# Expert items of 32 slots in four column tiles instead of 64 slots in two, rows gathered for four items at a time as before

## The reference, cut to what matters

```
def hierarchical_moe(xn, rg_w, rg_b, re_w, re_b, w1, w3, w2):
    ...
    g_top, g_idx = lax.top_k(g_prob, 1)                      # one of 4 groups
    ...
    e_top, e_idx = lax.top_k(jax.nn.softmax(e_logits), 2)    # two of its 8 experts
    e_w = e_top / jnp.sum(e_top, axis=-1, keepdims=True) * g_top
    ...
    h = jax.nn.silu(jnp.einsum('td,edf->tef', t, w1)) * jnp.einsum('td,edf->tef', t, w3)
    h = h * gate[:, :, None].astype(h.dtype)
    y = jnp.einsum('tef,efd->td', h, w2)
```

```
11  6  4  1 13  3 13  3 |  8  5  5  6 10 11  3 12
65 10 25 40 44 57 43 62 |  4  3  3 15  3  8  2 14
```

## Time and profile before

| | us |
|---|---|
| median of 3 runs | 1420.75 (1420.71 to 1421.07) |
| span of the profiled execution | 1421.0 |
| TensorE busy / DVE / ACT / GpSimd | 1355.8 / 537.2 / 347.3 / 228.6 |
| moved from HBM | 468.95 MB |

### The profile page before, as it was taken

One profiled execution on the slowest core, in us unless ns is written; L12 is line 12 of the kernel. 1 busy time (PEld: TensorE's weight loads), 2 busy tenths in 40 slices (PEclk: granted clock), 3 DMA queues, 4 the chain that ended last, 5 costly groups with the idle time before them and its releaser, 6 DMA issues.

```text
span 1421.0 us, 19044 instructions
## 1 busy us (share of the span) xinstructions
PE 1355.8 (95%) x7236; PEld 766.4 (54%) x7236; DVE 537.2 (38%) x1017; ACT 347.3 (24%) x623; POOL 228.6 (16%) x205
## 2 busy tenths in 40 slices
PE   7999999999999999998998999999999999898987
PEld 7884898987786345444433533544544543443533
DVE  6999420544425233233313323223323331331315
ACT  1121378566571111110210110111111121111003
POOL 2002756687881000000000000000000000000000
PEclk9999999999999999999999999999999999999999
DMA  8433543434475999999999999959999999999993
GB/s 214 178 119 119 208 178 119 155 142 161 140 292 235 384 428 428 427 428 427 428 429 428 429 428 428 428 224 429 428 428 428 428 428 428 429 428 428 428 425 138
DMA packets 71540, 471.76 MB, mean 332 GB/s; under 512 B 17329, under 2 KB 17410, under 8 KB 46274
## 3 DMA queue, kind: packets, MB, share of 16 engines
q1 hardware_dynamic: 70834, 469.75, 80.5%
q10 hardware_dynamic: 528, 1.05, 0.2%
q0 software_dynamic: 128, 0.26, 0.1%
HBM read 468.95 MB, written 2.10 MB: 331 GB/s over the span
## 4 chain that ended last, share of the span: by engine, by line
PE 62%; DMA 19%; DVE 2%; ACT 1%; issue 1%; POOL 1%; DVEq 0%; POOLq 0%; SPq 0%; ACTq 0%
PE ps L1932 24%; DMA ring<-in_expert_w_dram 18%; PE ps L1950 12%; PE ps L1590 11%; PE ps L1910 5%; PE ps L1940 3%; PE ps L1968 2%; PE ps L1969 1%; DMA reg_e<-in_expert_w_dram 1%; POOL w_lo L570 1%; PE ps L1922 1%; PE ps L1857 0%; DVE reg_x L1518 0%; DVE reg_y L1134 0%; PE ps L1764 0%
## 5 line engine op out<-in xcount | busy, mean ns | idle before, releaser
L1950 PE MATMUL ps<-ring,reg_y 128*64 128x512 f32 x1056 | 241.8, 611 | 14.1 <-issue 7.4
L570 POOL TENSOR_TENSOR w_lo<-ring,w_hi 128x512 fp32r<-128x512 f32 x152 | 199.8, 1347 | 72.5 <-ACT w_hi L632 71.3
L1950 PEld LDWEIGHTS ps<-ring,reg_y 128*64 128x64 f32 x1056 | 76.0, 140 | 153.0 <-issue 148.4
L1407 DVE TENSOR_TENSOR y_lo_t<-ps,y_hi_t 64x512 fp32r<-64x512 f32 x128 | 88.2, 689 | 171.6 <-ACT y_hi_t L866 169.6
L866 ACT ACTIVATE y_hi_t<-ps 64x512 fp32r<-64x512 f32 x132 | 78.0, 591 | 279.9 <-PE ps L1950 278.3
L1415 DVE TENSOR_TENSOR reg_x<-ps,reg_x 128x512 f32<-128x512 f32 x128 | 82.2, 684 | 152.3 <-PE ps L1969 152.3
L1932 PE MATMUL ps<-reg_e,reg_s 128*64 128x512 f32 x528 | 119.4, 594 | 10.5 <-POOLq L595 10.5
L1932 PE MATMUL ps<-ring,reg_s 128*64 128x512 f32 x528 | 120.0, 596 | 7.2 <-POOLq L595 6.7
L1396 DVE TENSOR_SCALAR reg_y<-ps,lamv 128x512 f32<-128x512 f32 x33 | 24.8, 751 | 269.0 <-PE ps L1932 269.0
L1932 PE MATMUL ps<-ring,reg_y 128*64 128x512 f32 x528 | 119.9, 596 | 5.5 <-POOLq L595 5.0
L1932 PE MATMUL ps<-reg_e,reg_y 128*64 128x512 f32 x528 | 119.4, 594 | 3.8 <-POOLq L595 2.3
(11 more groups left out here) (405 smaller groups left out, 1759.9 us busy)
## 6 DMA issues: line engine op xcount, KB each, us to landing
ring<-in_expert_w_dram SPq DMA_DIRECT2D x128, 2048.0 KB, 20.1
reg_e<-in_expert_w_dram SPq DMA_DIRECT2D x64, 2048.0 KB, 20.5
ring<-in_w_in_dram SPq DMA_DIRECT2D x19, 2048.0 KB, 7.6
ring<-in_w_out_dram SPq DMA_DIRECT2D x8, 2048.0 KB, 7.9
reg_x<-in_x_dram SPq DMA_DIRECT2D x4, 1024.0 KB, 8.3
ring<-in_w_in_dram SPq DMA_DIRECT2D x2, 1024.0 KB, 7.3
out_dram<-reg_x SPq DMA_DIRECT2D x3, 512.0 KB, 2.7
reg_e<-in_ssm_w_glu_dram ACTq DMA_DIRECT2D x1, 1024.0 KB, 8.6
```

Source lines behind the costliest of these rows:

```text
L570: G.tensor_tensor(w_lo[:, i % BUFS, :], unit(u % SLOTS_A)[:, c, :], w_hi[:, i % BUFS, :], ALU.subtract).then_inc(row_lo, 1)
L1407: V.tensor_tensor(y_lo_t[64 * q:64 * q + 64, w], psb[3 + k // 2][64 * (k % 2):64 * (k % 2) + 64, :], y_hi_t[64 * q:64 * q + 64, w], ALU.su ...
L1950: last = M(psb[3 + i // 2][64 * (i % 2):64 * (i % 2) + 64, :], hT[:, 2 * half + f, :], unit2(s)[:, f, 512 * i:512 * i + 512], start=half = ...
```

## The change

SLOT becomes 32 and QE becomes 4, so a matmul of `up` and `down` has M = 32 and goes to one of four column tiles (PSUM partitions 0, 32, 64, 96) instead of one of two. QG stays at 4: a group now has 4 times 32 = 128 gathered slots, in place of 256, and an iteration is the same as a group (HG = 1). The result of `down` fits in one bank (3). A token count of 33 or more needs a second item: with the counts above 39 items instead of 33 (expert 16 three, experts 19 to 23 two each). EXTRA, the bound on the items beyond 32, goes from 8 to 16. In the order by hand `pe_head` is gone; gather and gates of the next group stand between the turn and the down of a group's last item. `a_down` waits for the whole down instead of its first half.

```
-SLOT = 64
+SLOT = 32
+IOTA = 64
 QE = P // SLOT
 QG = 4
...
-EXTRA = 8
+EXTRA = 16
...
             def a_down(i_, n_, q):
-                a.wait_ge(e_dn, n_ + 1)
+                a.wait_ge(slot_free, used(n_, 6))
                 a.wait_ge(e_comb, i_ * 8 + 1)
                 for k in range(4):
...
-                    A.activation(y_hi_t[64 * q:64 * q + 64, 512 * k:512 * k + 512],
-                                 psb[3 + k // 2][64 * (k % 2):64 * (k % 2) + 64, :], cp).then_inc(e_yhi, 1)
+                    A.activation(y_hi_t[SLOT * q:SLOT * q + SLOT, 512 * k:512 * k + 512],
+                                 psb[3][SLOT * k:SLOT * k + SLOT, :], cp).then_inc(e_yhi, 1)
...
 (up)
-                        i = c % 2
-                        last = M(psb[m][64 * i:64 * i + 64, :], xeT[half][:, c, 64 * q:64 * q + 64], unit(s)[:, c, :],
-                                 start=cc < 2, stop=cc >= DC - 2)
+                        i = c % QE
+                        last = M(psb[m][SLOT * i:SLOT * i + SLOT, :], xeT[half][:, c, SLOT * q:SLOT * q + SLOT], unit(s)[:, c, :],
+                                 start=cc < QE, stop=cc >= DC - QE)
...
 (down_half)
+                for f in range(2):
+                    for i in range(4):
+                        last = M(psb[3][SLOT * i:SLOT * i + SLOT, :], hT[:, 2 * half + f, :],
+                                 unit2(s)[:, f, 512 * i:512 * i + 512],
+                                 start=half == 0 and f == 0, stop=half == 1 and f == 1)
                 last.then_inc(slot_free, 1)
             def down(n_):
                 pe.wait_ge(e_h, n_ + 2)
+                pe.wait_ge(e_ylo, n_ * 4)
                 down_half(n_, 0)
                 down_half(n_, 1)
...
+            def pe_items(i_, g_, n0, h, first=False, last=False, tail=False):
+                pe_up(i_, g_, n0, h, first)
+                down(n0)
+                for q in range(1, QE):
+                    n_ = n0 + q
+                    up(n_, QE * h + q, 0, (0, 1))
+                    up(n_, QE * h + q, 1, (0, 1))
+                    turn(n_)
+                    if last and q == QE - 1:
+                        next_gather(i_ + 1, g_ + 1)
+                        next_gates(i_ + 1, g_ + 1, 1 if tail else QG)
+                    down(n_)
...
             pe_up(i_last, extra + (GROUPS - 1), n_last, 0)
             pe.wait_ge(e_h, n_last + 2)
-            down_half(n_last, 0)
             pe.wait_ge(e_stev, i_last + 1)
-            for c in range(2):
+            for c in range(3):
                 last = M(psb[FIN_BANK[0, c]][:, :], ident_r[:, :], h_hi[:, 0, 0:4, :].rearrange("p c t -> p (c t)"), start=True, stop=True)
             last.then_inc(f_clear, 1)
-            down_half(n_last, 1)
+            down(n_last)
```

More of the change, by code:

```diff
@@ L360, in build @@
         f_rt = sem("f_rt")
-        e_dn = sem("e_dn")
         f_clear = sem("f_clear")
@@ L850, in a_silu @@
                 a.wait_ge(e_h, n_ + 1)
-                A.activation(hs, psb[2][:, 0:256], ACT.Silu).then_inc(e_silu, 1)
+                A.activation(hs, psb[2][:, 0:EC * SLOT], ACT.Silu).then_inc(e_silu, 1)
             def a_up(g_, n_, q):
@@ L1493, in _ @@
             v.wait_ge(f_clear, 1)
[L1494 to L1503, removed]
+            for c in range(3):
+                v_residual(c)
+            v_down(n_last, 0)
+            v.wait_ge(e_ylo, n_last * 4 + 4)
+            v_residual(3)
             def f_mean(b):
@@ L1920, in gates @@
                     for b in range(TB):
-                        for k in range(2):
-                            last = M(psb[7][64 * k:64 * k + 64, 2 * q:2 * q + 2], selS[:, b, q, :].bitcast(F), rg[:, b, q, :],
+                        for k in range(QE):
+                            last = M(psb[7][SLOT * k:SLOT * k + SLOT, 2 * q:2 * q + 2], selS[:, b, q, :].bitcast(F), rg[:, b, q, :],
                                      start=b == 0 and q == 0, stop=b == 1, skip_group_check=True)
@@ L1997, in pe_up @@
                 slots_to_rows(i_, h)
-            def pe_second(n_, q):
-                up(n_, q, 0, (0, 1))
-                up(n_, q, 1, (0, 1))
-                turn(n_)
-            def pe_items(i_, g_, n0, h, first=False):
-                pe_up(i_, g_, n0, h, first)
-                down(n0)
-                pe_second(n0 + 1, QE * h + 1)
-            def second_down(n_):
-                pe.wait_ge(e_ylo, n_ * 4)
-                down(n_)
-            def pe_group(g_, first=False):
-                for h in range(HG):
-                    pe_items(g_ * HG + h, g_, g_ * QG + QE * h, h, first and h == 0)
-                    if h < HG - 1:
-                        second_down(g_ * QG + QE * h + 1)
             def next_gather(i_, g_):
@@ L2025, in next_gates, with pe_group @@
                 gates(g_, nq)
-            def pe_head(g_):
-                next_gather(g_ * HG, g_)
-                next_gates(g_ * HG, g_, QG)
-                second_down(g_ * QG - 1)
+            def pe_items(i_, g_, n0, h, first=False, last=False, tail=False):
+                pe_up(i_, g_, n0, h, first)
+                down(n0)
+                for q in range(1, QE):
+                    n_ = n0 + q
+                    up(n_, QE * h + q, 0, (0, 1))
+                    up(n_, QE * h + q, 1, (0, 1))
+                    turn(n_)
+                    if last and q == QE - 1:
+                        next_gather(i_ + 1, g_ + 1)
+                        next_gates(i_ + 1, g_ + 1, 1 if tail else QG)
+                    down(n_)
+            def pe_group(g_, first=False, tail=False):
+                for h in range(HG):
+                    pe_items(g_ * HG + h, g_, g_ * QG + QE * h, h, first and h == 0, h == HG - 1, tail)
             keep_clock(3, psb[7], xt[:, 0, 0:512])
```

108 lines of the change are left out of this document (39 added, 69 removed).

## The result

The changed kernel takes 1505.2 us (median of 4 runs, 1498.5 to 1508.8) where the kernel before takes 1420.8: a ratio of 1.0588, 95% interval 1.0559 to 1.0618. Slower, as forecast, but by 84 us and not by 40, and outside the range of 1440 to 1488. The profiled execution has a span of 1496.8 us.

The account below looks back on a forecast made before the run. Expert stage bound by bringing in 403 MB by DMA, landings 4.90 us apart. 1421.0 - 6.7 (start) + 43.2 (double items) + 14 (clock) - 10.5 (end) = 1461 us, range 1440 to 1488.

Parts of the forecast that it names:

- loss = gap + 2.5: At a hole in the weight transfers: the loss is the gap from last landing to next issue, plus 2.5 us for restart.
- Part 1: Expert matmuls with M = 32: four tiles run at once, a unit takes 1.72 us, a non-first item 13.2 instead of 23.6.
- Part 2: Start: expert 1's k0 and k1 are issued sooner, its last unit lands near 485.4, -6.7 us (bounds -2 and -8).
- Part 3: Experts with further items: six waits from k5's landing to the next issue cost 59.0 us in place of 15.8, +43.2.
- inner pairs: Experts 19, 21, 23, both items inside one group: 6.3 us lost each, 18.9 together.
- outer pair: Experts 20 and 22, items across a group's end with the gather between turn and down: 10.3 us lost each, 20.6 together.
- Part 4: TensorE at the lower clock at most k5 landings: 2.0 us at each of seven places, +14 (bounds 0 and 20).
- Part 5: Last seven items, groups of one: 28 us of work in 29.4, so TensorE is there when the last unit lands.
- The end: From the last landing to the span's end: 19.0 us instead of 29.5, -10.5 (bounds -12 and -4).
- Rival B: Last loop: branch cost of 5.4 us a turn makes six items take 34 instead of 29.4; 1490 us, chance 0.08.
- A: Expert matmuls: at most two streams at a time, unit 3.43 us, item 23.5; about 1555 us, chance 0.10.
- C: Routing gives few other experts over 32, so start and end outweigh expert 16's loss: 1411 us, faster, chance 0.08.

Follow-up runs that it names:

- wide gather: The changed kernel with each gather matmul streaming its 128 slots twice (256 columns, second copy to unused columns of the bank): 1459.1 us, ratio 1.0267 to the kernel before.
- groups of eight: The changed kernel with QG = 8 instead of 4, so rows are gathered for eight items, 256 columns per gather matmul: 1461.1 us, ratio 1.0277 to the kernel before.

## Why the prediction was right in its direction and wrong in its size

- **What bounds the kernel; rule loss = gap + 2.5.** Right. Landings stay 4.90 apart outside the holes and the last loop; at expert 17 the gap was 18.5 (930.4 to 948.9) and the loss 20.7, so the restart cost 2.2.
- **Part 1, a unit of 1.72.** Right, and with it the 13.2 of an item (13.4). That PSUM's copies stay hidden was right too. The Trainium skill (TensorEngine Tiling (Array Packing), Theoretical Speedup) has up to 4x for tiles of 32, and these rows agree; by the 2.38 times of the Trainium skill (TensorE: Matmul & The Clock Gate, Why this matters for your kernels), as an estimate, a unit would be 2.2, and they don't.
- **Part 2, the start.** Mis-sized: -3.7 instead of -6.7, though inside its bounds. k0 went at 455.25 and not 452.8: the gather began at 448.2, 1.4 later than in the earlier trace rows, since the routing in front of it ran later in this trace, though the masks are narrower. In the wide gather, whose masks are the same, it began at 446.2.
- **Part 3 at the six places.** Right at four, and 59.0 in all where 69.0 came. The inner pairs lost 6.2 to 6.7 (6.3), expert 16 20.7 (19.5). The outer pair of expert 22 took 11.4 and not 10.3: its k3 unit ran at the lower clock, 3.22 us instead of 1.92. That of expert 20 took 17.7. Its k3 unit was as slow, and on top its gather runs from 1070.5 to 1082.5, 12.0 us, and its down takes 4.91 instead of 3.64, where the gather of expert 22 runs from 1153.4 to 1160.5, the 7.2 of the forecast. Windows of the changed kernel over both:

```profile
1072.50:1082.50 10.00, 10.00 (x48) 9.93 (x47) 2.54 (x6) 0.00 (x0) 0.00 (x0) 0.50 0.14 59
1157.00:1166.00 9.00, 8.94 (x142) 5.74 (x145) 2.53 (x7) 0.83 (x2) 0.00 (x0) 1.00 0.01 2
```

With the wide gather the two lose alike, 12.2 and 12.3.
- **Part 4, the clock at the landings.** Its 12 us at the six places turn the 59.0 into 71, close to the measured 69.0, and that is luck. By its mechanism the units at the k5 landings should run at the lower clock. At the three inner pairs the first half of down did (3.27 to 3.53 us), but TensorE was back at the higher clock when k5 landed, and so nothing was lost there. The half behind the landing of k5 of expert 19:

```profile
1039.40:1041.10 1.70, 1.70 (x16) 0.51 (x20) 0.00 (x0) 0.00 (x0) 0.00 (x0) 1.00 0.00 0
```

Of the 10 us beyond 59.0, 7.4 are at expert 20, most of them its slow gather, which this part named only in passing.
- **Part 5, "28 in 29.4".** This is the step that failed. Its gather of 7.2 us took the passes at 0.112; at 0.213 it would take 13.6, and the item 34.4. The rows have 32.7 and 35.3, with gathers of 11.9 and 13.9 and downs of 4.76 and 5.35 instead of 3.64, and six items lost 29.6 us. The change from "0 in the last loop" to 29.6 is the whole of the miss between 1461 and the profiled 1496.8, but for 6. The wide gather settles the cause: only the gather's columns differ (with their places in the bank), the clock comes back within it, and the loss is gone; groups of eight say the same. Part 4 did say "more if the gather runs cold too" and the range named it, but at a few us for seven places; I didn't put the cold gather into part 5, where a margin of 1.4 us decides, nor ask why TensorE should be at the higher level there.
- **The end.** Mis-sized by 3: 24.1 instead of 19.0 with 2 for the clock. With TensorE the bound, it is late at the last landing, by 4.4 us. The 5.4 us of the earlier trace rows, for which the forecast had 1.5, don't occur in the changed kernel: from 1240 us on its longest idle time is the 2.02 for the selection.
- **Rival B** forecast 1490 by items of 34 us. Its size was right and its cause wrong: it blamed the branches, of which three kernels with the same loop show nothing. Its chance of 0.08 was too low, because I weighed only the cause that I could name. **A** and **C** were wrong.
- **What stays open:** why the runs of the changed kernel are spread over 0.7% (the kernel before: 0.03% in the same comparison, 0.2% over all). Their mean granted clock goes with it, 0.872 in the run of 1498.5 us and 0.860 and 0.864 in those of 1508.5 and 1508.8, so more work at the lower clock is likely, but only the first was traced. And why the narrow gather keeps the higher clock at expert 22 and loses it at expert 20, with the same wait of 2.97 us in front of both.

## What to carry to other kernels

Where an item's time stands within a few per cent of the transfer beside it, work the item out at both of the clock's levels, and ask first for the stretch that consists of short passes. Fewer slots save streaming, but not the load of 128 columns of weights in each pass of the turn and the gather; a pass that streams 128 columns was bound by that load here, and widening it to 256 cost nearly nothing. When work is cut into smaller items on the same weights, count what each further item holds up: here 69 us at six places, which outweighs the 12 us that the narrower tiles gain without second items (one run each).

## What the runs showed of the hardware

- Float32 matmuls of 32 columns in four column tiles run four at a time: 1.72 us for 16 passes of 512 columns, 3.43 in two tiles.
- A pass with 128 columns of weights takes 0.112 us with 128 columns to stream and 0.119 with 256; at the lower clock 0.213 in both.
- TensorE fell to the lower clock while busy without a gap, in passes of 128 columns: to 0.50 at 1072.5, after 7.3 us without idle time, and it stayed there to the gather's end at 1082.5; again from 1410.5 to 1421.0. With 256 columns it also ran 2.4 us at 0.50, and then returned to 1.00 in the same gather.
- More work took less time: with twice the columns in every gather the kernel was 46 us (3%) faster, 39.6 by the profiled spans.
- The restart of a dry queue cost 2.2 to 2.5 us beyond the gap.
